# Two layer borders: four weight tiles held on either side and multiplied with one half of the tokens, then the other

## The chip, the core and the metric

One core of one Trainium2 chip runs the whole program. The metric is the device time of one execution in microseconds. TensorE (PE; its weight loads are listed as PEld), VectorE (DVE), ScalarE (ACT), GpSimd (POOL) and the queue of SyncE (SP) each work through their own instructions in order and wait for one another on semaphores.

## The reference

Four layers work in fp32 on one batch of S = 256 tokens of width D = 2048. What matters here is what stands between the output product of one layer and the input product of the next:

```
layers 0 and 1:   h = layernorm(x) * (1 + scale) + shift;   p = h @ w_in[l]
                  y_f = fourier_mix(u_f) * silu(z_f);       y_a = mla_attention(...) * silu(z_a)
                  y = concat([y_f, y_a]) @ w_out[l]
                  x = layernorm(ALPHA * x + gate * y, ln_g[l], ln_b[l])
layer 2 (even):   p = rms_norm(x, even_norm) @ even_w_in;   ...   x = x + y @ even_w_out
layer 3 (odd):    p = rms_norm(x, odd_norm) @ odd_w_in;     ...   x = x + y @ odd_w_out
```

So two norms follow one another behind layer 0 (the closing layernorm, then the opening one of layer 1), and two behind layer 1 (the closing layernorm, then the rms norm of layer 2). A token's norms need that token's 2048 values only.

## The kernel before

The token block lies in X as two halves of 128 tokens, t = 0 and t = 1. A weight matrix streams through in jobs: each is one tile of 256 rows by 512 columns (512 KB), loaded into one of 9 staging tiles `stg` by the SP queue. A "split" makes of it a high part `whi` (ACT, a rounding copy to fp32r; 4 buffers, NSPLIT) and a low part `wlo` (DVE, the difference). PE then takes three products per tile, high·high, high·low and low·high (fp32r), and adds them up in PSUM. Eight jobs q = 0..7 make one group (`group`, line 205) and run through the 2048 rows of the contraction.

Units of kind A (first groups of a layer) keep a 128x128 piece of the weight in the array and stream all 256 tokens of Hh or Hl past it: 24 matmuls of 256 columns per job. Units of kind B (`w_out`) keep 128 tokens in the array and stream 512 weight columns: 12 matmuls per job, 6 for each half of the tokens. Hh and Hl are the high and low part of the transposed, normed input.

The order is written by `Plan`. `run` (line 174) prepares job i (load and split are put into the queues) and then issues the matmuls of job i - 3 (AHEAD). Every engine takes the steps of that one list, in its order, and skips those that are not its own.

At a border, in the order of the list:

- `out` of the last group (line 2136): for t = 0 and then 1 the PSUM result times the gate, plus ALPHA·x, then bn_stats, on DVE.
- `post_norm` (lines 381, 1775, 1783, 2111): the aggregate and a reciprocal square root by three Newton steps on small columns, for both halves together (`meanvar`, `rsqrt`), then for each half three DVE passes over X. Behind layer 0 ACT meanwhile computes sum and sum of squares of half 0; behind layer 1 it squares both halves.
- `ln` or `rms` (lines 2072, 2091): the statistics of the next norm, both halves together.
- `xn` (lines 1766, 2099): the normed values by quarters of 512 columns, half 0 on DVE, half 1 on ACT, into XN, which lies over Z.
- `trans` (lines 346, 1734, 2049): PE transposes 2 x 2 blocks of 128x128 for both halves (line 1533); scale and shift are applied from PSUM on ACT or DVE, ACT writes Hh, DVE writes Hl.
- `lead` (line 992) puts this first part with three transposed steps in front of the first job of the next layer, and one more transposed step (`more`) in front of each of its jobs 1 to 5. The first eight jobs are "fresh": their products with Hh come first, and those with Hl last.

The steps `ln_load`, `mla_begin` and `even_begin` put DMAs into POOL's queue; they are not changed.

Of the kernel before, what the change touches and what calls it, by code (L numbers as in the profile page):

```python
# [16 lines left out]
D = 2048  # L17
S = 256
KT = D // 128
EPS = 1e-6  # L20
# [9 lines left out]
AHEAD = 3  # L30
WINDOW = 6
# [10 lines left out]
PT2X = dict(even=(IQ, IQ + 384), odd=(V3 + 512, KS3 + 512))  # L42

# [18 lines left out]
class Plan:  # L62
# [3 lines left out]
    def __init__(self):  # L66
# [9 lines left out]
        self.starting = True  # L76
        self.retired = []
# [78 lines left out]
    def prep(self, job):  # L156
        slot, free = self.stgs.get()
        while not self.starting and slot >= NSTG:
            self.retired.extend(free)
            slot, free = self.stgs.get()  # L160
# [4 lines left out]
        if job["mode"] == "split":  # L165
            hi, hfree = self.his.get()
            job["hi"] = hi
            a, b = self.tick("hi"), self.tick("lo")
            self.step("split", slot=slot, n=job["n"], hi=hi, ld=ld, hfree=hfree, hi_done=a)
            job["split"] = b  # L170
        elif job["mode"] == "ada":
            job["dve"](job)

    def run(self):
        n = len(self.jobs)
        held, weights = [], 0
        for i in range(n + AHEAD):
# [6 lines left out]
            if i < n:  # L184
                if job.get("last_chunk"):
                    self.starting = False
                self.prep(job)
                held.append(job)
# [3 lines left out]
            while weights > AHEAD or self.starting and len(held) > AHEAD:  # L192
# [12 lines left out]
    def group(self, cols, units, post, pre=None, late=None, early=None):  # L205
        g = {}
        n = sum(c[2] for c in cols)
        for q in range(8):
# [5 lines left out]
            def body(job, q=q):  # L214
                if q == 0:
                    g["pair"], g["free"] = self.pairs.get()
                tok = self.tick("mm")
                here = early is not None and q < 2
                self.step("mm", q=q, early=early if here else None, pair=g["pair"], free=g["free"] if q == 0 else (), split=job["split"],
                          hi=job["hi"], slot=job["slot"], units=units, h=[self.y_early[q]] * 2 if here else [self.h[2 * q], self.h[2 * q + 1]],  # L220
                          h_hi=[self.h_hi[2 * q], self.h_hi[2 * q + 1]] if job.get("fresh") else None)
                self.his.put(job["hi"], tok)
                self.stgs.put(job["slot"], tok)
                g["mm"] = tok
# [9 lines left out]
            self.jobs.append(dict(mode="split", src=src, n=n, mm=body, pre=pre if q == 0 else late if q == 3 else None,  # L234
# [126 lines left out]
    def ln(self, x, post=None):  # L361

        s = dict(mv=self.small(4), v=self.small(2), y=self.small(2), nb=self.small(1), t=self.small(2), nbt=self.tick("nb"))
        self.step("ln", x=x, post=post, **s)
        self.norm = dict(how="ln", ready=s["nbt"], y=s["y"], mv=s["mv"], nb=s["nb"], nm=post["nm"] if post else None)
# [15 lines left out]
    def post_norm(self, l):  # L381
        tk = [self.tick("post_norm") for _ in range(4)]
        s = dict(l=l, ln=self.ln_in, x=self.x[1, 3], mv=self.small(4), v=self.small(2), y=self.small(2), t=self.small(2),
                 z_free=self.z_free, out=tk)
        if l == 0:
            s.update(sum=self.small(1), nm=self.small(1), sq=self.small(1))
            s["summed"], s["mean"], s["squared"] = self.tick("pn_sum"), self.tick("pn_mean"), self.tick("pn_sq")
        else:
            s["ss"] = self.small(4)
            for _ in range(4):  # L390
                s["squared"] = self.tick("sumsq")
        self.ar = (tk[3],)
        self.h_free = self.mm_last
        return self.step("post_norm", **s)
# [48 lines left out]
    def out_post(self, l, g):  # L443
        def post(pair, mm):
            free = []
            for t in range(2):
                a = self.tick("out_in")
                free.append(a)
                s = dict(l=l, g=g, t=t, pair=pair, mm=mm)
                if l < 2:  # L450
# [5 lines left out]
                    self.x[t, g] = st  # L456
                elif l == 2:
# [11 lines left out]
    def w_out(self, l, w):  # L469
        for g in range(4):  # L470
            def late(g=g):
                if g == 0:
                    self.y_rest()
                    if l < 2:
                        self.ln_in = self.tick("ln_landed", 32)
                        self.step("ln_load", l=l, scores=("score_mm", self.count["score_mm"]))
                    if l == 2:
                        self.toep = self.tick("toep_landed", 96)
                        self.step("toep_windowed", logits=("sm_logit", self.count["sm_logit"]), pool=self.pool_mm)
            self.group([(w, g * 512, 512)], B2, self.out_post(l, g), late=late, early=l)  # L480
# [534 lines left out]

    def whole(self):
# [58 lines left out]
        def norm1():  # L1075
            p = self.post_norm(0)
            self.ln(p["out"][3], p)

        n1 = self.lead(norm1, lambda qs: self.mod_h(1, qs), lambda: self.mla(1))
# [6 lines left out]
        def norm2():  # L1086
            p = self.post_norm(1)
            self.rms(p["squared"], p["ss"], 4)

        self.lead(norm2, lambda qs: self.transposed("en", None, qs), self.even)  # L1090
# [48 lines left out]
def build(nc, A):  # L1139
    with ExitStack() as ctx:  # L1140
# [18 lines left out]
        whi = [sb(f"whi{i}", [128, 2, 512], F32R) for i in range(NSPLIT)]  # L1159
        X = sb("X", [128, 2, D])  # L1160
# [8 lines left out]
        for whole, tiles in ((AR, stg), (ARL, wlo)):  # L1169
            tiles += [whole[:, 3072 + i * 1024:4096 + i * 1024].rearrange("p (k n) -> p k n", k=2) for i in range(EXTRA)]  # L1170
        RX = sb("RX", [128, 768])
# [181 lines left out]
        def tensor(e):  # L1353
# [7 lines left out]
            for kind, s in plan.order:  # L1361
                if "bank" in s and kind != "setup":
                    B = PB[s["bank"]]
                if kind == "mm":
# [51 lines left out]
                    ins.then_inc(SEM["mm"], 1)  # L1416
                elif kind == "direct" and s["split"] is None:
# [285 lines left out]
        def scalar(e):  # L1703
# [7 lines left out]
            for kind, s in plan.order:  # L1711
# [54 lines left out]
                elif kind == "xn":  # L1766
# [3 lines left out]
                    if s["how"] == "ln":  # L1770
                        ins = act(XN[:, 1, cols], X[:, 1, cols], ACT.Identity, bias=sm(s["nb"], 1), scale=sm(s["y"] + 1, 1))
# [3 lines left out]
                elif kind == "post_norm" and s["l"] == 0:  # L1775
# [7 lines left out]
                elif kind == "post_norm":  # L1783
                    q.wait_ge(s["z_free"])
                    for n in range(4):
                        t, cols = n // 2, slice(1024 * (n % 2), 1024 * (n % 2) + 1024)
# [659 lines left out]
```

## Time and profile before

| | |
|---|---|
| median of 3 runs | 1639.75 us (1638.62 to 1642.59) |
| profiled execution | 1637.07 us, its span 1635.3 us |
| PE busy | 1508.8 us (92%) |
| DVE busy | 1086.4 us (66%) |
| ACT busy | 706.7 us (43%) |
| mean granted clock of TensorE | 0.965 of full speed |

The profiled execution has its own time, a little below the median; a sum from its rows is made against 1637.07 us. Times of rows are counted from the start of the span. A matmul's listed duration (0.28 us, say) includes its way through the array; how often one starts is read from the difference of two starts.

### The profile page before, as it was taken

How to read it: one execution, taken by the hardware profiler on the slowest of the kernel's cores; microseconds unless marked ns; L12 is line 12 of the kernel's file. 1: busy time of each engine (PE TensorE's matmuls, PEld its weight loads, DVE VectorE, ACT ScalarE, POOL GpSimd, SP SyncE). 2: the span in 40 equal slices, each digit the busy share in tenths (PEclk: the TensorE clock that was granted, in tenths of full speed). 3: DMA queues.
4: the chain of work that ended last, by engine and by line, in shares of the span. 5: the costliest groups of instructions: out<-in, count | busy, mean ns of one | idle time of the engine just before them, and what ended most of it. 6: DMA issues, size and time to landing. Idle time of an engine off the chain costs nothing.

```text
span 1635.3 us, 25215 instructions
## 1 busy us (share of the span) xinstructions
PE 1508.8 (92%) x9919; PEld 1329.6 (81%) x9919; DVE 1086.4 (66%) x1854; ACT 706.7 (43%) x1195; POOL 30.7 (2%) x56
## 2 busy tenths in 40 slices
PE   4888999989949999999968999999998999999998
PEld 0667788988839888998858998789987998879986
DVE  3426668889987757666676466884655667886553
ACT  1324234335326444444325344544544545655442
POOL 3000000000000000000000000010000000000000
PEclk8898999999979999999988999999999999999999
DMA  9996887998945766676546546427665553434662
GB/s 351 380 380 230 256 288 252 368 330 331 346 155 170 255 168 200 226 244 207 193 141 197 174 142 177 133 73 262 184 193 153 167 155 104 115 106 140 183 218 90
DMA packets 182437, 345.00 MB, mean 211 GB/s; under 512 B 28876, under 2 KB 43440, under 8 KB 181552
## 3 DMA queue, kind: packets, MB, share of 16 engines
q1 hardware_dynamic: 177744, 326.88, 61.7%
q0 software_dynamic: 4576, 16.52, 2.9%
q8 instruction: 78, 1.28, 0.3%
q14 instruction: 39, 0.32, 0.1%
HBM read 341.16 MB, written 2.20 MB: 210 GB/s over the span
## 4 chain that ended last, share of the span: by engine, by line
PE 78%; DVE 8%; DMA 5%; ACT 4%; issue 3%; SPq 2%; POOLq 0%; POOL 0%; DVEq 0%; ACTq 0%
PE PM L1359 65%; PE PB L1359 8%; DMA stg<-in_w_in 3%; SPq L1284 2%; ACT AR L1709 2%; DMA AR<-in_w_in 1%; ACT whi L1709 1%; DVE X L1934 1%; PE PB L1561 1%; PE PB L1533 1%; DVE AC L1934 1%; PE PB L1636 1%; DMA AR<-in_w_ada 1%; DVE wlo L2010 1%; DVE AR L1934 1%
## 5 line engine op out<-in xcount | busy, mean ns | idle before, releaser
L2010 DVE TENSOR_TENSOR wlo<-stg,whi 128x1024 fp32r<-128x1024 f32 (+2 forms) x421 | 500.1, 1197 | 350.3 <-ACT whi L1709 349.0
L1709 ACT ACTIVATE whi<-stg 128x1024 fp32r<-128x1024 f32 (+2 forms) x421 | 434.2, 1037 | 467.4 <-PE PM L1359 352.2
L1359 PE MATMUL PM<-Hh,whi 128*128 128x256 f32 x1824 | 528.0, 292 | 9.1 <-DVE wlo L2010 6.6
L1359 PE MATMUL PM<-Hh,wlo 128*128 128x256 f32 x1780 | 501.5, 285 | 0.0
L1359 PE MATMUL PM<-Hl,whi 128*128 128x256 f32 x1824 | 498.1, 285 | 0.0
L1359 PEld LDWEIGHTS PM<-Hh,whi 128*128 128x128 f32 x1824 | 353.2, 194 | 28.8 <-issue 12.4
L1359 PEld LDWEIGHTS PM<-Hh,wlo 128*128 128x128 f32 x1780 | 344.1, 193 | 0.0
L1359 PEld LDWEIGHTS PM<-Hl,whi 128*128 128x128 f32 x1824 | 343.1, 193 | 0.6
L1359 PE MATMUL PM<-whi,Hh 128*128 128x512 f32 (+1 forms) x576 | 224.3, 391 | 0.0
L1359 PE MATMUL PM<-wlo,Hh 128*128 128x512 f32 (+1 forms) x576 | 220.9, 385 | 0.0
L1359 PE MATMUL PM<-whi,Hl 128*128 128x512 f32 (+1 forms) x576 | 219.1, 385 | 0.0
L1934 DVE SCALAR_TENSOR_TENSOR AC<-stg,CA,AC 128x1024 f32<-128x1024 f32 x120 | 153.7, 1281 | 9.3 <-DMA stg<-in_w_ada 7.2
L1359 PEld LDWEIGHTS PM<-whi,Hh 128*128 128x128 f32 x576 | 108.9, 189 | 22.2 <-issue 0.7
L1359 PEld LDWEIGHTS PM<-wlo,Hh 128*128 128x128 f32 x576 | 108.8, 189 | 20.8 <-issue 0.2
L1359 PEld LDWEIGHTS PM<-whi,Hl 128*128 128x128 f32 x576 | 107.4, 189 | 22.0
L1359 PE MATMUL PM<-whi,ARL 128*128 128x512 f32 (+1 forms) x272 | 86.0, 383 | 0.0
L1709 ACT ACTIVATE AR<-PB 128x384 f32<-128x384 f32 (+2 forms) x104 | 45.7, 478 | 91.9 <-PE PB L1636 31.1
L1359 PE MATMUL PB<-AR 64*128 64x256 f32 (+4 forms) x576 | 72.8, 359 | 5.0 <-ACT AR L1709 4.5
L1533 PE MATMUL PB<-IDN,Z 128*128 128x128 f32 x128 | 24.1, 333 | 57.4 <-DVE Z L2105 26.5
L1533 PEld LDWEIGHTS PB<-IDN,Z 128*128 128x128 f32 x128 | 18.5, 172 | 60.5 <-DVE Z L2105 26.7
L1359 PEld LDWEIGHTS PB<-AR 64*128 64x128 f32 (+2 forms) x576 | 47.3, 174 | 22.8 <-issue 7.9
L1359 PEld LDWEIGHTS PM<-whi,ARL 128*128 128x128 f32 x272 | 51.1, 188 | 10.0
(268 smaller groups left out, 1461.3 us busy)
## 6 DMA issues: line engine op xcount, KB each, us to landing
stg<-in_w_ada SPq DMA_DIRECT2D x162, 512.0 KB, 6.5
stg<-in_w_in SPq DMA_DIRECT2D x107, 512.0 KB, 5.4
stg<-in_even_w_in SPq DMA_DIRECT2D x80, 512.0 KB, 3.6
stg<-in_odd_w_in SPq DMA_DIRECT2D x72, 512.0 KB, 3.7
stg<-in_w_out SPq DMA_DIRECT2D x64, 512.0 KB, 5.0
stg<-in_even_w_out SPq DMA_DIRECT2D x32, 512.0 KB, 3.9
stg<-in_odd_w_out SPq DMA_DIRECT2D x32, 512.0 KB, 4.2
AR<-in_w_ada SPq DMA_DIRECT2D x30, 512.0 KB, 11.5
```

The lines of the kernel that those rows point to most:

```text
L1284: e.dma_start(dst, src).then_inc(SEM[f"landed{slot}"], 16)
L1359: return e.matmul(out, l, r, start=start, stop=stop, skip_group_check=True)
L1533: ins = e.transpose(B[:, kk * S + t * 128:kk * S + t * 128 + 128], XN[:, t, k * 128:(k + 1) * 128], IDN[:, :])
L1561: ins = e.matmul(B[:, 0:S], ar(UU + t * 1024 + s["g"] * 128, 128), CSS[:, t, :], start=t == 0, stop=t == 1)
L1636: ins = e.transpose(B[:, n * 128:(n + 1) * 128], L[:, n * 128:(n + 1) * 128], IDN[:, :])
L1709: return e.activation(out, x, f, **k)
L1934: return e.scalar_tensor_tensor(out=out, in0=in0, scalar=scalar, in1=in1, op0=op0, op1=op1)
L2010: e.tensor_tensor(wlo[s["slot"]][:, :, 0:n], stg[s["slot"]][:, :, 0:n], whi[s["hi"]][:, :, 0:n].bitcast(F32), ALU.subtract).then_inc(SEM[" ...
```

## The change

At the borders behind layers 0 and 1:

- In the last group of `w_out` the jobs 4 to 7 multiply with half 0 alone (`units[0:1]`), and their four tiles stay held. When job 7 has done so, the four are multiplied with half 1. The `out` steps of the two halves wait for different matmuls, and each half has its own `post_stat` and `post_norm`.
- The first four jobs of the next layer do no 256-column products. `first_half` multiplies them with half 0 of Hh, then (all four) with half 0 of Hl, then transposes half 1, multiplies all four with half 1 of Hh, and with half 1 of Hl: 192 matmuls of 128 columns instead of 96 of 256. Transposed steps 4 and 5 are issued inside, 6 and 7 in front of jobs 4 and 5.
- `lead_halves` replaces `lead`: `half_xn` and `half_trans` cover 512 columns of one half. For half 0 ACT writes XN, Hh, and a second copy into TMP from which DVE makes Hl; for half 1 DVE writes XN and reads PSUM itself.
- `half_norm` computes the next norm's statistics of one half at a time.
- From job 3 of `w_out`'s first group until job 7 of the next layer four more `whi` buffers (in ARL) and two more staging tiles (in AR, with their `wlo` in ARL) are in use. Behind job 7 of the last group the matmuls are issued one job later than usual (`later`).

In the last group of `w_out` of layers 2 and 3 job 7 alone is done this way (hold=1), and `out` of half 0 waits for its first part.

```diff
+            while not self.border and hi >= NSPLIT:
+                hi, hfree = self.his.get()
...
-            while weights > AHEAD or self.starting and len(held) > AHEAD:
+            while weights > AHEAD + (held[0]["later"] if held and "later" in held[0] else 0) or self.starting and len(held) > AHEAD:
...
+                    return self.first_half(job, q, g, units)
...
+                if q < 8 - hold:
+                    self.his.put(job["hi"], tok)
+                    self.stgs.put(job["slot"], tok)
+                else:
+                    g["held"].append((job, s))
+                if hold and q == 7:
+
+                    first = tok
+                    for job, s in g["held"]:
+                        tok = self.tick("mm")
+                        self.step("mm", **{**s, "units": units[1:2]})
+                        self.his.put(job["hi"], tok)
+                        self.stgs.put(job["slot"], tok)
+                    g["mm"] = [first, tok]
+                else:
+                    g["mm"] = tok
                 self.mm_last = tok
 
...
+        self.step("post_stat", **s)
+        if t == 1:
+            self.half_norm(0)
+        self.step("post_norm", **s)
+        h["out", t] = out
...
+        h = self.half
+
+        def part(job, q, t, lo):
+            tok = self.tick("mm")
+            self.step("mm_half", q=q, t=t, lo=lo, pair=g["pair"], free=g["free"] if q == 0 and t == 0 and not lo else (),
+                      split=job["split"], hi=job["hi"], slot=job["slot"], units=units, h=h["lo" if lo else "hi", t, q // 2])
+            return tok
+
+        g["held"].append((job, q))
+        part(job, q, 0, False)
+        if q < HELD - 1:
+            return
+        for j, k in g["held"]:
+            part(j, k, 0, True)
+        self.half_trans(1, 0)
+        self.half_trans(1, 1)
+        for j, k in g["held"]:
+            part(j, k, 1, False)
+        self.more(4)
+        for j, k in g["held"]:
+            tok = part(j, k, 1, True)
+            self.his.put(j["hi"], tok)
+            self.stgs.put(j["slot"], tok)
+        self.more(5)
+        self.mm_last = g["mm"] = tok
 
 
 
...
-                s = dict(l=l, g=g, t=t, pair=pair, mm=mm)
+                s = dict(l=l, g=g, t=t, pair=pair, mm=mm[t] if g == 3 else mm)
...
+                    if g == 3:
+                        self.post_norm(l, t)
...
+                        self.border = True
+                        self.his.free = [f for f in self.his.free if f[0] < NSPLIT]
+                        self.stgs.free = [f for f in self.stgs.free if f[0] < NSTG + EXTRA]
+                        for i, at in enumerate(HI_MORE[l]):
+                            self.his.put(NSPLIT + 4 * l + i, *idle)
+                        for i in range(len(STG_MORE)):
+                            self.stgs.put(NSTG + EXTRA + i, *idle)
...
+                       hold=0 if g < 3 else HELD if l < 2 else 1)
...
+        def lead():
+            l, h = self.half["l"], self.half
+            self.half_xn(0, 0)
+            self.half_trans(0, 0)
+            self.half_xn(0, 1)
+            self.half_trans(0, 1)
+            self.half_norm(1)
+            self.half_xn(1, 0)
+            self.half_xn(1, 1)
+            self.norm = dict(how="ln" if l == 0 else "rms", ready=h["tok"][1], y=h["y"], mv=h["mv"], nb=h["nb"])
+            self.more = more
+            begin()
+
+        def more(q):
+            if q % 2 == 0:
+                self.normed((q // 2,))
+            trans((q,))
+            if q == 7:
+                self.zw = self.h[KT - 1]
+        self.jobs[n]["pre"] = lead
+        for q in range(8):
+            self.jobs[n + q]["half" if q < HELD else "fresh"] = True
+        for q in (4, 5):
+            self.jobs[n + q]["pre"] = lambda q=q: more(q + 2)
+        self.jobs[n + 7]["border_end"] = True
+        return n
+
     def whole(self):
...
+                    for kk in range(2):
+                        k = 2 * s["q"] + kk
+                        opened = set()
+                        for u in s["units"]:
+                            b = PM[2 * s["pair"] + u["bk"]]
+                            first = k == 0 and s["t"] == 0 and not s["lo"] and u["bk"] not in opened
+                            opened.add(u["bk"])
+                            out = b[0:u["n"], u["off"] + s["t"] * 128:u["off"] + s["t"] * 128 + 128]
+                            wh, wl = (W[:, kk, u["c0"]:u["c0"] + u["n"]] for W in (H, L))
+                            if s["lo"]:
+                                ins = mm(out, wh, Hl[:, k, tk], False, False)
+                            else:
+                                mm(out, wh, Hh[:, k, tk], first, False)
+                                ins = mm(out, wl, Hh[:, k, tk], False, False)
+                    ins.then_inc(SEM["mm"], 1)
+                elif kind == "half_trans":
...
+                    for j in range(4):
+                        ins = affine(Hh[:, 4 * s["c"] + j, tk], j)
+                    ins.then_inc(SEM["h_hi"], 1)
+                    if s["t"] == 0:
+                        q.wait_all(s["tfree"])
+                        for j in range(4):
+                            ins = affine(TMP[s["tmp"]][:, j * 128:(j + 1) * 128], j)
+                        ins.then_inc(SEM["tr_half_act"], 1)
...
+                elif kind == "post_norm" and s["l"] == 1:
+                    t = s["t"]
...
+                    for n in range(2):
+                        cols = slice(1024 * n, 1024 * n + 1024)
...
+                        act(XN[:, t, cols], X[:, t, cols], ACT.Square, accum_out=sm(s["ss"] + 2 * t + n, 1)).then_inc(
+                            SEM["sumsq"], 1)
...
+                elif kind == "half_trans":
+                    T, k0, tk = TMP[s["tmp"]], 4 * s["c"], slice(s["t"] * 128, s["t"] * 128 + 128)
+                    q.wait_ge(s["hh"])
...
+                        ins.then_inc(SEM["tr_half_dve"], 1)
+                    q.wait_ge(s["aff"])
+                    q.wait_ge(s["h_free"])
+                    e.tensor_tensor(Hl[:, k0:k0 + 4, tk], T[:, :].rearrange("p (k s) -> p k s", k=4),
+                                    Hh[:, k0:k0 + 4, tk].bitcast(F32), ALU.subtract).then_inc(SEM["h_lo"], 1)
```

The lines that are left out of the diff are the new buffers' places, the small columns of the statistics, and the DVE code of `post_stat`, `half_norm` and `half_xn`, which does on one half what `meanvar`, `ln`, `rms` and `xn` did on two.

## Rows read from the trace of the kernel before

**Rows 1.** The page, section 1: busy us, share of the span, instructions.
```profile
PE 1508.8 (92%) x9919; PEld 1329.6 (81%) x9919; DVE 1086.4 (66%) x1854; ACT 706.7 (43%) x1195; POOL 30.7 (2%) x56
```

**Rows 2.** PE's waits: engine, line, waited for; total us, times, longest.
```profile
PE PB L1533 <- DVE Z L2105: 26.5, 4, 20.9
PE PB L1533 <- DVE Z L2109: 22.7, 2, 22.5
```

**Rows 3.** Stretches: length; PE, PEld, DVE, ACT, POOL busy; clock, DMA share, GB/s.
```profile
462.80:468.20 5.40, 5.40 (x24) 4.13 (x22) 2.02 (x4) 1.06 (x1) 0.00 (x0) 1.00 0.67 225
468.20:490.70 22.50, 0.03 (x2) 0.04 (x1) 21.20 (x45) 5.00 (x6) 0.90 (x1) 0.58 0.18 54
490.70:495.50 4.80, 4.80 (x23) 4.78 (x24) 2.84 (x6) 3.38 (x7) 0.00 (x0) 0.50 0.00 0
495.50:519.80 24.30, 24.11 (x203) 23.94 (x203) 19.25 (x25) 15.15 (x22) 0.00 (x0) 1.00 0.56 161
...
867.60:893.10 25.50, 25.03 (x211) 24.86 (x211) 18.16 (x24) 15.45 (x23) 0.00 (x0) 1.00 0.70 218
```

**Rows 4.** Timeline of DVE behind layer 0: start, duration, what.
```profile
468.26 0.69 DVE L2144 TENSOR_TENSOR TMP<-PM,GT 128x512 f32<-128x512 f32 x1 [0.34 <-PE PM L1359]
...
472.49 0.39 DVE L1996 BATCH_NORM_AGGREGATE SM<-STA 128x2 f32<-128x24 f32 x2
...
475.17 9.65 DVE L1934 SCALAR_TENSOR_TENSOR X<-X,SM,AR 128x2048 f32<-128x2048 f32 x6
484.85 2.47 DVE L2077 BATCH_NORM_STATS2 STA<-X 128x6 f32<-128x512 f32 x4
...
490.00 1.00 DVE L2109 TENSOR_SCALAR Z<-X,SM 128x512 f32<-128x512 f32 x2
```

**Rows 5.** Timeline of ACT behind layer 0.
```profile
480.12 1.91 ACT L1709 ACTIVATE Z<-X 128x2048 f32<-128x2048 f32 x1 [13.46 <-DVE X L1934]
...
484.30 0.19 ACT L1709 ACTIVATION_READ_ACCUMULATOR Z<-X,SM 128x1 f32 x1
490.00 1.52 ACT L1709 ACTIVATE Z<-X,SM 128x512 f32<-128x512 f32 x2 [5.51 <-DVE SM L1934]
491.81 1.02 ACT L1709 ACTIVATE Hh<-PB,MOD 128x256 fp32r<-128x256 f32 x2 [0.30 <-PE PB L1533]
```

**Rows 6.** Timeline of ACT behind layer 1.
```profile
860.20 1.06 ACT L1709 ACTIVATE Z<-X 128x1024 f32<-128x1024 f32 x1
...
863.88 1.33 ACT L1709 ACTIVATE Z<-X,SM 128x512 f32<-128x512 f32 x2 [2.54 <-DVE SM L1934]
865.59 0.84 ACT L1709 ACTIVATE Hh<-PB,VEC 128x256 fp32r<-128x256 f32 x2 [0.38 <-PE PB L1533]
```

**Rows 7.** Timeline of PE: matmuls that stream 1, 128 and 256 columns.
```profile
460.78 1.84 PE L1359 MATMUL PB<-ONE,AC 128*128 128x1 f32 x16
...
490.69 2.79 PE L1533 MATMUL PB<-IDN,Z 128*128 128x128 f32 x12 [22.47 <-DVE Z L2109]
...
498.16 0.28 PE L1359 MATMUL PM<-Hh,wlo 128*128 128x256 f32 x1
498.28 0.28 PE L1359 MATMUL PM<-Hh,whi 128*128 128x256 f32 x1
...
507.44 0.60 PE L1533 MATMUL PB<-IDN,Z 128*128 128x128 f32 x4
```

**Rows 8.** Weight loads by shape, whole span: count, busy us, mean ns, idle.
```profile
L1359 PEld LDWEIGHTS PM<-Hh,whi 128*128 128x128 f32 x1808 | 350.8, 194 | 28.8 <-issue 12.4 <-DVE wlo L2010 11.5 <-DVE ARL L2010 4.3
...
L1359 PEld LDWEIGHTS PB<-AR 128*64 128x64 f32 x192 | 11.8, 136 | 7.4 <-issue 1.7 <-DVE AR L1934 0.7
```

**Rows 9.** Timeline of ACT and DVE: the split of one tile in layer 1.
```profile
500.91 1.05 ACT L1709 ACTIVATE whi<-stg 128x1024 fp32r<-128x1024 f32 x1
...
501.98 1.23 DVE L2010 TENSOR_TENSOR wlo<-stg,whi 128x1024 fp32r<-128x1024 f32 x1 [0.26 <-ACT whi L1709]
```

**Rows 10.** Timeline of DVE at the end of the kernel.
```profile
1628.60 1.29 DVE L2151 TENSOR_TENSOR X<-PM,X 128x512 f32<-128x512 f32 x2 [8.50 <-PE PM L1359]
```

More of the change, by code:

```diff
@@ L157, in prep @@
         slot, free = self.stgs.get()
-        while not self.starting and slot >= NSTG:
-            self.retired.extend(free)
+        while not self.starting and NSTG <= slot < NSTG + EXTRA or not self.border and slot >= NSTG + EXTRA:
+            if slot < NSTG + EXTRA:
+                self.retired.extend(free)
             slot, free = self.stgs.get()
@@ L203, in run, with group @@
                     self.round()
-    def group(self, cols, units, post, pre=None, late=None, early=None):
-        g = {}
+    def group(self, cols, units, post, pre=None, late=None, early=None, hold=0):
+        g = dict(held=[])
         n = sum(c[2] for c in cols)
@@ L232, in done @@
                     self.pair_put(g["pair"], *free)
-            self.jobs.append(dict(mode="split", src=src, n=n, mm=body, pre=pre if q == 0 else late if q == 3 else None,
+            self.jobs.append(dict(mode="split", src=src, n=n, mm=body, later=1 if hold == HELD and q == 7 else 0, pre=pre if q == 0 else late if q == 3 else None,
                                   post=done if q == 7 else None))
@@ new lines, in half_norm, with half_xn @@
+    def half_norm(self, t):
+        h = self.half
+        h["tok"][t] = self.tick("nb")
+        self.step("half_norm", t=t, l=h["l"], y=h["y"], nb=h["nb"], mv=h["mv"], nm=h["nm"], sq=h["sq"], ss=h["ss"],
+                  squared=h.get("squared") if h["l"] == 0 else h["squared", t], out=h["out", t],
+                  v=self.small(1), w=self.small(1))
+    def half_xn(self, t, c):
+        h = self.half
+        self.step("half_xn", t=t, c=c, l=h["l"], y=h["y"], nb=h["nb"], mv=h["mv"], ready=h["tok"][t], z_free=self.z_free)
+        h["xn", t, c] = self.tick(f"half_xn{t}")
@@ new lines, in half_trans @@
+    def half_trans(self, t, c):
+        h = self.half
+        b, fr = self.now(self.banks)
+        mm = self.tick("tr_mm")
+        i, ifree = self.now(self.tmps)
+        hh = self.tick("h_hi")
+        a = self.tick("tr_half_act") if t == 0 else self.tick("tr_half_dve")
+        lo = self.tick("h_lo")
+        need = [self.mod[1, 4 + c], self.mod[1, c]] if h["l"] == 0 else []
+        self.step("half_trans", t=t, c=c, how="mod" if h["l"] == 0 else "en", bank=b, free=fr, src=h["xn", t, c], mm=mm, tmp=i,
+                  tfree=ifree, need=need, aff=a, hh=hh, h_free=self.h_free)
+        self.banks.put(b, a)
+        self.tmps.put(i, lo)
+        h["hi", t, c], h["lo", t, c] = hh, lo
```

199 lines of the change are left out of this document (138 added, 61 removed).

## The prediction

> **What bounds the kernel now.** The page first: PE is busy for 92% of the span, DVE for 66% [rows 1]. So time is won only where PE stands still, and lost where PE gets more to do. The list of waits then says where PE stands still: two waits on the normed input, 22.5 us behind layer 0 and 20.9 us behind layer 1 [rows 2]. The table by stretches shows both sides of the first: DVE busy for 21.2 of 22.5 us, PE not at all, and behind it the first eight jobs of the next layer packed: PE busy for 24.1 of 24.3 us and for 25.0 of 25.5 us [rows 3]. The reader is to see that such a wait is one chain on DVE, and that there is no slack behind it into which more PE work could go. The clock falls in the wait, and is back at full 4.8 us after PE resumes.
>
> **How I count.** F is the moment at which job 7 of `w_out`'s last group has done half 0. The pass of half 1 over four tiles is 24 matmuls of 512 columns, 5.4 us [rows 3], so PE's last old work ends at F+5.4, where it ends today. The weights don't hold it up: with eight `whi` buffers the splits run ahead. A split takes 1.05 us on ACT and 1.23 on DVE [rows 9], a tile now 1.36 us of PE; this edit I price at nothing, and at up to 2 us a border if DVE is late with one.
>
> **The first half's chain, layer 0.** DVE: `out` of half 0 takes half of 468.26 to 472.49, 2.15. Aggregate and Newton steps take 472.49 to 475.17, 2.7 for both halves; these are tiny columns, so one half costs nearly the same, 2.5. Three passes over X: half of 9.65, 4.85 [rows 4]. That is F+9.5. ACT's sum and square then take 480.12 to 484.49, 4.4 [rows 5]; DVE meanwhile does `out` and `post_stat` of half 1, to F+14.15. `half_norm(0)`, 2.5: F+16.7. XN by ACT, 0.76: F+17.5. So PE waits 12.1 us instead of 22.5. But its next two steps are both transposes, and the second needs XN of the second quarter, which ACT writes only after four copies to Hh and four to TMP. A copy of 256 columns takes 0.5 us here [rows 5], of which I give 0.35 to one of 128. From 490.69, the first transpose, to 491.81, the first copy, are 1.1 us. So F+17.5 + 1.1 + 8 x 0.35 + 0.8 = 22.2; the first four transposes end at F+18.4 (0.21 each), so there is a new wait of 3.9 us between the two groups of four. Products start at F+23, T+17.5 if T is the end of the old work; today at T+24.9.
>
> **Layer 1 is worse.** Here ACT squares both halves, and the squares of half 1 stand in its queue ahead of `half_xn(0, 0)`. They wait for DVE's last pass over X: F+14.15 + 2.4 (`half_norm(0)`) + 4.85 = 21.4, and the last one takes 1.06 [rows 6] and a read of 0.19 [rows 5]: F+22.7. Behind this wait stands all that ACT has for the new layer: XN, both sets of copies, the splits of jobs 4 to 6. XN 0.67: F+23.4. PE waits 18.0 us, today 20.9, and then 3.5 between the transposes (1.1 + 8 x 0.32 + 0.67, less 0.85 of transposing).
>
> **More PE work.** Each border has 192 matmuls of 128 columns for 96 of 256. One of 256 starts each 0.12 us [rows 7]. None of 128 in fp32r is in the trace. The lower bound is proportion: 0.053 for the columns at 2.4 GHz and the 0.013 that the 256 show above theirs, 0.067. The upper one is a start each 0.213, as 128-column transposes do at the low clock: (2.79 - 0.45) / 11 [rows 7]. The nearest rows say 0.11: 16 matmuls of one column take 1.84 us, so that an almost empty one still costs 0.105 to 0.112, and four transposes of 128 columns start 0.109 apart [rows 7]. The load of the array explains it: 128 columns of weights take 58 ns longer than 64 [rows 8], so about 0.116 for all 128, and each of the 192 loads another piece. With 256 columns the load hides under the stream, with 128 it no longer can. I take 0.112: 192 x 0.112 - 96 x 0.12 = 21.5 - 11.5 = +10.0 us a border. The Trainium skill ("TensorE: Matmul & The Clock Gate", section "Back-to-back issue gap") gives about 81 ns for a stream of load and matmul at N = 128. By that the term would be +4.0; no row here shows 81, and those that come near show 105 to 112.
>
> **New waits inside.** (a) Between the transposes of half 1 and their copy to Hh: 0.27 + 4 x 0.35, less 0.44 for the second four, 1.2 us (layer 1: 1.1). (b) Step 6 stands in front of job 4, behind the split of job 7 in the list, and PE has nothing left but it. Behind step 5's transposes come on ACT the scale and shift (0.95), Hh (0.6), the split of job 7 (1.05), XN; on DVE Hl, the split (1.2), XN (0.54): 0.3 + 0.95 + 0.6 + 1.05 + 1.2 + 0.54 = 4.6 us (layer 1: 4.4), after which PE can transpose for job 4. Nothing on PE covers it. (c) DVE does Hl of half 0, `half_norm(1)` (484.85 to 490.00, 5.15 [rows 4]) and two XN to F+33.1; PE comes for them at F+35, so they are hidden, by about 2 us. With faster matmuls they would not be. The splits of jobs 4 to 6 on DVE (3.5 us) and a first `ada` product end before Hl of half 1 is wanted.
>
> **Clock.** It falls in any wait of this length here; today about 20 matmuls run at the low clock per border, then about as many (8 transposes, 14 narrow ones, at 0.213). Difference nothing; if it doesn't come back, rival C.
>
> **The other edits.** The DMAs keep their order; POOL's wait for the last X, now T+16 against T+17. The held tiles free their staging late, but eleven exist: jobs 7 and on have theirs 20 us early. At the ends of layers 2 and 3 `out` of half 1 no longer stands behind that of half 0: 1.29 us for two [rows 10], 0.6 gained at each, -1.2.
>
> **Sum.**
> - Layer 0: waits 12.1 + 3.9 + 1.2 + 4.6 = 21.8, today 22.5 + 0.2; work +10.0: +9.1.
> - Layer 1: waits 18.0 + 3.5 + 1.1 + 4.4 = 27.0, today 20.9 + 0.5; work +10.0: +15.6.
> - Ends: -1.2.
> Together +23.5: from 1637.07 to 1660.6 us in the profiled execution's terms. The median is 2.7 above that execution: 1663.3, say 1663.
>
> **Rivals.**
> A, the forecast, +23.5: 70%, its own range 1653 to 1673.
> B, a narrow matmul costs by its columns, 0.067. Against it the one-column row; for it, that no fp32r one is shown. Work falls to +1.4 a border, but PE then outruns DVE: about 2 us more of wait (c), 1 of Hl. Layer 0 +3.2, layer 1 +7.2, ends -1.2: +9.2, 1649. 14%. By the 81 ns of the Trainium skill (same page and section) it would be about +13, 1653.
> C, the narrow ones start each 0.213, because the clock stays low under them or for another reason. The 12 transposes and 23 matmuls after 490.7 did raise it [rows 3]. 2 x (192 - 14) x 0.1 = +36: 1699. 6%.
> D, faster. The place is the inside waits: 3.9, 1.2, 4.6 and 3.5, 1.1, 4.4, 18.7 us in all. If the steps that I put behind one another in ACT's queue (second copy, split, XN) are over before PE asks, and the columns alone count (work +2.8 instead of +20): 23.5 - 18.7 - 17.2 = -12.4: 1627 by the median. With all waits gone it decides from 0.10 us a matmul down. For it: these waits rest on my reading of one list; against: all are in one engine's order. 5%.
> E, the two sides cancel, 1640: half of D. 5%.
>
> **Numbers.** What a measurement of this kernel tells from no change is about 0.3%, 5 us. Faster: D's 5 and 1 of E, 6%; same: the other 4 of E and 1 of B, 5%; slower 89%. The range takes in B and large parts of A's misses above, and leaves out C and D: 1644 to 1680.
>
> **What would show it.** PE's first wait behind layer 0 near 12 us and behind layer 1 near 18, each followed by one of about 4 between two groups of transposes; narrow matmuls 0.11 apart, with PEld nearly full; a wait of about 4.5 us in front of step 6's transposes. I am wrong if these start 0.07 apart, if ACT's XN of half 0 behind layer 1 comes before its squares of half 1, or if the clock stays at half.

## The result, and the profile after

The changed kernel takes 1703.4 us (median of 4 runs, 1701.4 to 1704.1), the one before 1641.2 in the same comparison (1638.6 to 1642.7): ratio 1.038, interval 1.036 to 1.040. I had forecast 1663 with a range of 1644 to 1680. The direction is right, the size is 40 us off, and the time is that of rival C (1699), to which I had given 6%.

The head of the page of the kernel after, to be laid beside [rows 1]: PE has 63 us more of busy time (1572.2 for 1508.8), nearly all of the 65 us by which the span is longer.

```profile
span 1700.7 us, 25673 instructions
## 1 busy us (share of the span) xinstructions
PE 1572.2 (92%) x10111; PEld 1390.7 (82%) x10111; DVE 1092.1 (64%) x1908; ACT 712.7 (42%) x1225; POOL 30.7 (2%) x56
```

The list of PE's waits of the kernel after, first behind layer 0 (460 to 540 us), then behind layer 1 (865 to 960); columns: us in total, times, longest. They answer to [rows 2].

```profile
PE PB L1572 <- ACT Z L1866: 15.8, 2, 12.0
PE PB L1690 <- DVE Z L2343: 4.5, 1, 4.5
PE PM L1488 <- ACT Hh L1866: 0.7, 1, 0.7
...
PE PB L1572 <- ACT Z L1866: 20.4, 2, 17.4
PE PB L1690 <- DVE Z L2341: 4.3, 1, 4.3
PE PM L1488 <- ACT Hh L1866: 0.4, 1, 0.4
```

So behind layer 0 PE waits 12.0, 3.8, 0.7 and 4.5 us (forecast 12.1, 3.9, 1.2, 4.6), behind layer 1 17.4, 3.0, 0.4 and 4.3 (forecast 18.0, 3.5, 1.1, 4.4). The waits aren't where the 40 us are. The table by stretches of the kernel after shows where; its columns are the stretch, its length, busy us of PE, PEld, DVE, ACT, POOL with their instructions, the granted clock, DMA share, GB/s. Layer 0's border: the products of half 0, those of half 1, the wide jobs behind them. Then the same three behind layer 1. Beside [rows 3].

```profile
485.10:508.30 23.20, 22.46 (x106) 22.06 (x106) 10.56 (x25) 7.52 (x17) 0.00 (x0) 0.50 0.08 22
509.50:530.50 21.00, 20.95 (x99) 20.55 (x98) 4.75 (x10) 1.25 (x3) 0.00 (x0) 0.50 0.20 51
535.90:549.00 13.10, 13.10 (x103) 13.10 (x103) 7.65 (x10) 4.71 (x7) 0.00 (x0) 0.92 0.36 105
...
895.20:917.90 22.70, 22.32 (x106) 21.92 (x105) 7.09 (x20) 6.46 (x17) 0.00 (x0) 0.50 0.28 94
918.80:939.90 21.10, 21.10 (x100) 20.79 (x99) 4.34 (x10) 1.03 (x2) 0.00 (x0) 0.50 0.17 50
945.20:958.50 13.30, 13.30 (x104) 13.30 (x104) 5.94 (x7) 5.25 (x8) 0.00 (x0) 0.91 0.42 119
```

The clock is 0.50 (1.2 GHz) under all narrow products, 99 in 21.0 us: one each 0.212, where the forecast had 0.112. It is at the low level from 469.8 for 68 us and from 876.0 for 72 us; before, for 24 and 21 us. It returns only under the wide products, as the timeline of PE in the kernel after shows (start, us, line, operation):

```profile
486.20 0.41 PE L1488 MATMUL PM<-Hh,ARL 128*128 128x128 f32 x1
486.41 0.41 PE L1488 MATMUL PM<-Hh,wlo 128*128 128x128 f32 x1
...
534.98 1.09 PE L1690 MATMUL PB<-IDN,Z 128*128 128x128 f32 x4 [4.53 <-DVE Z L2343]
535.72 0.56 PE L1488 MATMUL PM<-Hh,whi 128*128 128x256 f32 x1
...
537.57 0.41 PE L1488 MATMUL PM<-Hh,whi 128*128 128x256 f32 x1
537.78 0.41 PE L1488 MATMUL PM<-Hh,wlo 128*128 128x256 f32 x1
...
538.30 0.28 PE L1488 MATMUL PM<-Hh,whi 128*128 128x256 f32 x1
538.42 0.28 PE L1488 MATMUL PM<-Hh,wlo 128*128 128x256 f32 x1
```

Narrow products (128 streamed columns) and wide ones (256) start equally far apart at the low clock, 0.21. The clock is back at 538.1, 2.4 us after the first wide one, and the starts are 0.12 apart again.

### The profile page after: what moved, and what is told of

Its sections match the earlier page's. It is cut to its first block, busy times and chain, and to the rows that moved or that the text cites. A ratio compares the mean times of both kernels' runs of the same rounds, so it can differ in the third digit from the quotient of the medians.

```text
span 1700.7 us, 25673 instructions
## 1 busy us (share of the span) xinstructions
PE 1572.2 (92%) x10111; PEld 1390.7 (82%) x10111; DVE 1092.1 (64%) x1908; ACT 712.7 (42%) x1225; POOL 30.7 (2%) x56
## 4 chain that ended last, share of the span: by engine, by line
PE 77%; DVE 8%; DMA 5%; ACT 5%; issue 3%; SPq 2%; POOLq 0%; POOL 0%; DVEq 0%; ACTq 0%
PE PM L1488 64%; PE PB L1488 8%; DMA stg<-in_w_in 3%; SPq L1413 2%; ACT AR L1866 2%; ACT whi L1866 1%; DVE AC L2125 1%; DVE X L2125 1%; PE PB L1690 1%; PE PB L1718 1%; DVE wlo L2201 1%; DMA stg<-in_w_out 1%; PE PB L1793 1%; DMA AR<-in_w_in 1%; DMA AR<-in_w_ada 1%
## 5 line engine op out<-in xcount | busy, mean ns | idle before, releaser
L2201 DVE TENSOR_TENSOR wlo<-stg,whi 128x1024 fp32r<-128x1024 f32 (+2 forms) x382 | 452.5, 1194 | 319.8 <-ACT whi L1866 319.1
L1866 ACT ACTIVATE whi<-stg 128x1024 fp32r<-128x1024 f32 (+2 forms) x382 | 393.4, 1036 | 414.3 <-PE PM L1488 317.4
L1488 PE MATMUL PM<-Hh,whi 128*128 128x256 f32 (+2 forms) x1792 | 525.8, 295 | 9.4 <-DVE wlo L2201 7.5
L1488 PE MATMUL PM<-Hh,wlo 128*128 128x256 f32 (+1 forms) x1804 | 525.2, 292 | 0.0
L1488 PE MATMUL PM<-Hl,whi 128*128 128x256 f32 (+2 forms) x1792 | 496.6, 287 | 0.0
L1488 PEld LDWEIGHTS PM<-Hh,whi 128*128 128x128 f32 (+1 forms) x1792 | 352.2, 197 | 29.2 <-DVE wlo L2201 12.6
L1488 PEld LDWEIGHTS PM<-Hl,whi 128*128 128x128 f32 (+1 forms) x1792 | 341.9, 196 | 0.6
L1488 PEld LDWEIGHTS PM<-whi,Hl 128*128 128x128 f32 x520 | 96.9, 189 | 19.7
L1488 PE MATMUL PM<-Hh,ARL 128*128 128x128 f32 (+1 forms) x180 | 61.7, 378 | 1.1 <-ACT Hh L1866 1.1
L1488 PE MATMUL PM<-whi,ARL 128*128 128x512 f32 (+1 forms) x176 | 55.5, 380 | 0.0
L1488 PE MATMUL PM<-wlo,ARL 128*128 128x512 f32 (+1 forms) x140 | 52.8, 377 | 0.0
```

The source lines that it names most:

```text
L1488: return e.matmul(out, l, r, start=start, stop=stop, skip_group_check=True)
L1866: return e.activation(out, x, f, **k)
L2201: e.tensor_tensor(wlo[s["slot"]][:, :, 0:n], stg[s["slot"]][:, :, 0:n], whi[s["hi"]][:, :, 0:n].bitcast(F32), ALU.subtract).then_inc(SEM[" ...
```

## Experiments

Theory: the waits and the price at the full clock were right, and narrow matmuls that start at the low clock leave it low. Rivals: 0.112 is wrong; the clock is kept down by the waits inside the border; the cost isn't PE's at all. Below, a kernel's extra time is counted against the kernel before as timed with it: the changed kernel has +62.2 us.

**1. The narrow matmul at the full clock.** In the kernel before, the second group of layer 2 (PE busy without a break) is multiplied in halves, with all 128 stationary columns in one kernel and 64 in the other; with 64, half of that group's outputs is left out.

```diff
+m = s["narrow"]                                 # 128 or 64
+for x, w in ((xh, wh), (xl, wh), (xh, wl)):
+    for h in range(2):
+        o, th = u["off"] + 128 * h, slice(128 * h, 128 * h + 128)
+        ins = mm(b[0:m, o:o + 128], w[:, 0:m], x[:, kk, th], ...)
```

> The kernel before, with one change far from the borders: in the second group of layer 2 (eight jobs, PE packed and at full clock today, 192 matmuls of 256 columns starting 0.12 us apart, 23.0 us) each product is done as two matmuls of 128 columns, 384 in all. Theory 1 (the load of the array sets the price, and the clock, once full, stays): a start each 0.112 us, 43.0 us, +20 us. Theory 1b (same price, but such matmuls also bring a full clock down): the stretch begins at 0.112 and goes over to 0.213, the granted clock falls within it, up to +59 us. Theory 2 (128 columns in fp32r cost 0.213 at any clock): 0.213 from the first one at granted clock 1.0, +59 us. Theory 3 (the columns count): 0.067, +3 us.

> As narrow_warm, but each of the 384 matmuls loads only 64 of the 128 weight columns, so half of this group's outputs aren't computed. Same number of matmuls and of streamed columns, half the load. If the load sets the price (theory 1): a start each 0.067 us or so, 26 us for the group, +3 us against before. If 128 streamed columns are slow by themselves: as narrow_warm, 0.11 or 0.213.

Measured: 1657.3 against 1637.2, ratio 1.013 (1.010 to 1.015), +20 us for 384 narrow ones in place of 192 wide; with 64 stationary columns 1638.1, ratio 1.000 (0.998 to 1.001). Stretches of the first kernel, then the timeline of the first and of the second:

```profile
895.00:914.00 19.00, 19.00 (x173) 19.00 (x172) 4.90 (x4) 4.01 (x4) 0.00 (x0) 1.00 0.22 45
914.00:938.00 24.00, 24.00 (x216) 24.00 (x216) 3.00 (x4) 4.07 (x7) 0.00 (x0) 1.00 0.19 39
```

```profile
914.78 0.39 PE L1359 MATMUL PM<-Hh,wlo 128*128 128x128 f32 x2
915.00 0.38 PE L1359 MATMUL PM<-Hh,whi 128*128 128x128 f32 x2
```

```profile
914.97 0.28 PE L1359 MATMUL PM<-Hh,wlo 128*64 128x128 f32 x2
915.08 0.28 PE L1359 MATMUL PM<-Hh,whi 128*64 128x128 f32 x2
```

A pair each 0.22, so 0.111 a narrow matmul, and 0.06 with half the stationary columns: the load sets the price, as the forecast had it. The clock stays at 1.00 for the 43 us of the narrow ones. The price of 0.112 stands, and with it the first rival falls.

**2. The changed kernel at the full clock.** 50 and 16 extra matmuls of 512 columns fill the first and second wait behind layer 0, 74 and 13 those behind layer 1; the transposes overwrite their result.

```diff
+hi, split, n = s["fill"]
+q.wait_ge(split)
+for _ in range(n):
+    mm(B[:, :], whi[hi][:, 0, 0:128], whi[hi][:, 0, :], True, True)
 q.wait_ge(s["src"])
```

> The changed kernel, with matmuls of 512 columns on a held weight tile put into PE's waits in front of the transposes of half 0 (50 and 16 behind layer 0, 74 and 13 behind layer 1; their result is overwritten by the transposes). They only keep PE busy. Theory 1: the clock is full when the narrow matmuls begin and stays there, these start 0.112 apart, and the time is what the prediction worked out, about 1660 us, less some 2 us a border for the slow starts that both kernels have. Theory 1b: it begins so and falls under them, 1670 to 1700. Theory 2 (narrow costs 0.213 at any clock): 1703 as it is.

Measured: 1657.7 against 1637.2, ratio 1.0135 (1.0115 to 1.0154). Stretches: the filled wait and the first products behind layer 0, and the filled wait behind layer 1.

```profile
466.30:478.50 12.20, 11.64 (x53) 9.35 (x52) 11.28 (x32) 5.12 (x6) 0.00 (x0) 1.00 0.31 101
485.00:498.00 13.00, 11.84 (x106) 11.60 (x106) 11.14 (x27) 7.61 (x16) 0.00 (x0) 1.00 0.09 32
...
849.00:867.00 18.00, 17.34 (x77) 14.04 (x77) 15.08 (x33) 5.20 (x9) 1.69 (x3) 1.00 0.26 87
```

The clock stays at 1.00 until 511, behind the last narrow product of layer 0's border, and until 897 at the other. PE does more work, and the kernel is 42 us nearer to the one before (+20.5 for +62.2). These +20.5 are close to the +23.5 of the sum.

**3. Wide products in halves.** The changed kernel with the operands' roles exchanged in the border: 128 tokens stationary, 512 weight columns streamed, 48 matmuls a border. Their result then has another layout, so what is computed from it is wrong; the order of the steps is that of the changed kernel.

```diff
-mm(out, wh, Hh[:, k, tk], first, False)
-ins = mm(out, wl, Hh[:, k, tk], False, False)
+mm(out, Hh[:, k, tk], H[:, kk, :], k == 0, False)
+ins = mm(out, Hh[:, k, tk], L[:, kk, :], False, False)
```

> The changed kernel with the same passes over the four held tiles at each border, but the operands' roles exchanged: 128 tokens stay in the array and 512 weight columns stream, 12 matmuls of 512 columns a tile instead of 48 of 128. The sums of these four tiles come out in another layout than the rest of their group, so the values behind are wrong; time, order and waits are those of the changed kernel. Theory 1: the clock comes back some 4 to 7 us into the first pass as it did before the change, the passes cost 11 us a border instead of 41, DVE's part becomes visible by 2 to 3 us, and the time is 1646 to 1655 us. If the passes' order or the held buffers and not the narrow matmuls were what keeps the clock low, it stays above 1685.

Measured: 1649.5 against 1637.2, ratio 1.0083 (1.0067 to 1.0100). The clock falls in the waits and comes back each time: under the first stretch at 487.8, 2.5 us behind the first product, as one starts each 0.43 us at first and then each 0.23. Mean clock of the first stretch of products and of the second:

```profile
485.00:495.00 10.00, 7.18 (x27) 5.59 (x26) 5.83 (x20) 5.74 (x11) 0.00 (x0) 0.84 0.19 52
498.00:507.00 9.00, 8.33 (x32) 6.30 (x32) 7.42 (x16) 2.46 (x6) 0.00 (x0) 0.81 0.07 11
```

The waits on ACT's XN are those of the changed kernel (36.2 us in four, longest 17.4, in both lists); one on DVE of 2.9 us is new, as expected. 50 us are gone (+12.3 for +62.2). Not all of that is the clock: at the full clock 48 products each 0.227 are 10.4 us a border less than 192 each 0.111, 21 us for two; the other 29 are what the clock costs, as far as this run tells.

**4. Packed narrow products at the low clock, without the change.** The kernel before, its chain and waits untouched, with only the first four tiles' products of both borders narrow; a second kernel with 64 of 128 stationary columns (half of these outputs left out).

```diff
+m = min(u["n"], s["narrow"])                    # narrow: 128 or 64
+for t in range(2):
+    mm(b[0:m, u["off"] + t * 128:u["off"] + t * 128 + 128], w[:, 0:m], Hh[:, k, t * 128:t * 128 + 128], ...)
```

> The kernel before, its chains and its 22.5 and 20.9 us waits as they are, but the products of the first four tiles behind layers 0 and 1 in 192 matmuls of 128 columns a border for 96 of 256 (same tiles, same order, no break between them). Theory 1: narrow matmuls that start at the low clock don't lift it, so it stays at 0.5 from the wait until the 256-column ones of the fifth tile have run for 2 to 3 us. Then 192 x 0.213 = 40.9 us for the 13.7 us that 23 x 0.213 + 73 x 0.12 take now, +27 a border, and some 1.2 us for 12 wide ones at the low clock: +28 a border, +56 in all, about 1693. Rival: in the changed kernel the clock stayed down because the block is broken by waits (4.0, 1.0, 4.7 us); here the block is packed, so the clock is back about 5 us after the work resumes, and a border costs 24 x 0.1 less 23 x 0.09 for the low part and 10 us for the rest: +10 to +11 a border, 1657 to 1660.

> The kernel before with its first four tiles' products behind layers 0 and 1 in 192 matmuls of 128 columns, as in the run with the packed narrow block, but with 64 of 128 stationary columns (so half of these outputs is left out). If the load of 128 stationary columns is what leaves the clock low, it comes back as in the kernel before, a start each 0.06, and the time is 1635 to 1640 where before takes 1638. If 128 columns of stream are too few by themselves, the clock stays low behind at least one border: 192 x 0.11 = 21 for 13.7 and 1.2 for the tail, +8.6 a border, 1647 (one border) to 1655 (both).

Measured with 128 stationary columns: 1654.0 in one execution, 1678.8, 1678.8 and 1680.1 in three, where before takes 1638.7. So +15 once and +40 three times, with a mean granted clock of 0.973 once and of 0.954 to 0.959 three times. The profiled one (1680.1) shows how they can differ. Stretches: the narrow block and the first wide products behind layer 0, then the narrow block behind layer 1.

```profile
493.90:537.20 43.30, 43.30 (x207) 43.30 (x206) 13.04 (x19) 11.01 (x17) 0.00 (x0) 0.50 0.14 43
537.90:541.00 3.10, 3.10 (x17) 3.10 (x16) 2.13 (x3) 0.90 (x2) 0.00 (x0) 0.50 0.49 127
541.00:548.00 7.00, 7.00 (x59) 7.00 (x59) 4.71 (x6) 3.52 (x6) 0.00 (x0) 0.97 0.52 154
898.60:922.00 23.40, 23.40 (x207) 23.40 (x206) 11.74 (x18) 10.25 (x16) 0.00 (x0) 0.97 0.51 166
```

The same block of the same program, PE busy from end to end in both: 43.3 us at one border, where the clock never rose under it, 23.4 at the other, where it was back 3.9 us after PE resumed with 12 transposes. So breaks aren't needed to keep the clock low, and the rival of the waits inside falls. Neither expectation holds whole: I had +56 for "it never lifts" and +21 for "it always lifts", and got +40 or +15. From the first transposes behind layer 0 to those behind layer 1 this execution takes 31.0 us longer than the kernel before (404.7 for 373.7), and from there to the end 11.0 (781.9 for 770.9): a low border costs 20 us more than one where the clock returns. The 1654.0 has no trace; that both its borders rose is an inference from its time and clock, and by the trace two such borders would cost 22, not 15.

With 64 stationary columns: 1636.4, ratio 1.000 (0.999 to 1.001), before 1637.7. The profiled execution, first products behind layer 0 and then those behind the rise of the clock:

```profile
495.11 0.41 PE L1360 MATMUL PM<-Hh,whi 128*64 128x128 f32 x2
495.32 0.41 PE L1360 MATMUL PM<-Hh,wlo 128*64 128x128 f32 x2
...
502.56 0.28 PE L1360 MATMUL PM<-Hh,whi 128*64 128x128 f32 x2
502.67 0.28 PE L1360 MATMUL PM<-Hh,wlo 128*64 128x128 f32 x2
```

At the low clock one starts each 0.107, half of the 0.213 with 128 columns, so there too the load sets the price. The clock returned at 497.4 and 869.3, 5.7 and 3.8 us after PE resumed. All 10 executions lie between 1633.3 and 1641.5, where I had reckoned 8.6 us for a border that stays low; so probably none did. With 128 stationary columns three of four did. That the load of all 128 is what leaves the clock low is likely by this, but not shown: one border with this load rose, and the two kernels ran on different chips.

**5. A kick.** The changed kernel with 16 extra matmuls of 512 columns, or 32 transposes of 128, in front of the first narrow product of each border.

```diff
+if s["q"] == s["t"] == 0 and not s["lo"]:
+    for _ in range(16):
+        mm(PM[2 * s["pair"]][:, :], H[:, 0, 0:128], H[:, 0, :], True, True)
...                                              # in the second kernel:
+    for _ in range(32):
+        e.transpose(PM[2 * s["pair"]][:, 0:128], IDN[:, :], IDN[:, :])
```

> The changed kernel with 16 extra matmuls of 512 columns (result unused) in front of the first narrow product of each border, behind both waits on the transposes; all waits are as in the changed kernel. Theory: what keeps the clock low is that narrow matmuls don't lift it, though they hold it once it is up. The 16 take up to 6.9 us at the low clock, lift it, and the 192 narrow ones then start 0.112 apart for 0.213: -19.4 + 6 to 7, and some 1.5 less in low transposes and in the wide ones behind: -14 a border, 1675 where the changed kernel took 1703. Rival: narrow matmuls between waits of 1 and 4.7 us can't hold it either: it falls back inside the block, and the time is 1703 + 12 less a part, 1695 to 1716.

> As the kernel with 16 wide matmuls, but 32 transposes of 128 columns of fp32 in their place (0.213 each at the low clock, 6.8 us). They start as far apart as the narrow products do. [...] Then they lift it, as the 12 in front of the products in the kernel before may do: 1675. Theory 2: any instruction that starts each 0.213 leaves the clock low: then 1703 + 13.6 = 1717.

Measured: 1679.6, ratio 1.0248 (1.0234 to 1.0262), and 1677.0 (1672.5 to 1688.8), ratio 1.0256 (1.0219 to 1.0293), before at 1637.7. Stretches behind layer 0: with wide kicks the kick, the narrow products of half 0, the 1.2 us in which PE waits for Hh, the products of half 1; then with transposes the kick and the products of half 0.

```profile
486.00:491.00 5.00, 5.00 (x20) 4.08 (x20) 1.76 (x3) 4.76 (x11) 0.00 (x0) 0.76 0.35 102
491.00:501.90 10.90, 10.90 (x100) 10.90 (x99) 8.55 (x22) 0.98 (x2) 0.00 (x0) 1.00 0.01 2
502.60:503.80 1.20, 0.14 (x1) 0.14 (x2) 0.16 (x1) 1.20 (x4) 0.00 (x0) 1.00 0.00 0
505.80:523.70 17.90, 17.90 (x86) 17.90 (x86) 4.05 (x9) 0.63 (x1) 0.00 (x0) 0.50 0.20 53
```

```profile
486.60:492.30 5.70, 5.70 (x33) 5.70 (x32) 2.42 (x5) 5.42 (x11) 0.00 (x0) 0.58 0.33 91
492.40:502.60 10.20, 10.20 (x94) 10.20 (x92) 7.79 (x20) 0.22 (x1) 0.00 (x0) 1.00 0.01 2
```

Both kicks lift it, the transposes at 491.3, 4.7 us behind the first of them. Extra work of 5 to 6 us halves the time of the 96 products behind it and brings the kernel 20 and 23 us nearer to the one before (+41.9 and +39.3 for +62.2); I had expected 28 (1675 for 1703). In the profiled run with wide kicks part of that is lost because the clock fell again at 505.5, 1.8 us after the small wait for Hh, and the 86 narrow ones behind it didn't bring it back, 0.1 us each. In the profiled run with transposes it didn't fall under either narrow block, and that one took 1673.0; two of its other three took 1681.0 and 1688.8, and no trace shows why. My rival (they can't hold it past a wait) is right for layer 0's border under the wide kick, and wrong for the one behind layer 1, where it stood at 1.00 from 891.2 to 921.8.

**6. The w_out side alone.** The change's held last tiles and its `out`, statistics and post norm by halves; the next layer's norm, transposes and products as before, 256 wide. In a second kernel the norm of half 0 is no step of its own but one with half 1's. In both the matmuls are no longer issued one job later (`later`).

```diff
-            self.half_xn(0, 0)
-            self.half_trans(0, 0)
...
-            self.half_xn(1, 1)
...
+        n = self.lead(norm, trans, layer, fill)   # norm: half_norm(1); then both halves at once
...
-        if t == 1:
-            self.half_norm(0)                     # these two in the second kernel only
```

> The change's w_out side alone: the last four tiles of layers 0 and 1 (one tile in layers 2 and 3) are held and multiplied with half 0, then half 1, and each half's out, statistics and post norm start when it is done; the next layer's norm and its first products are for both halves at once, 256 columns wide, as before. By the chain that the prediction wrote (F+14.15 for half 1's out and statistics, +2.5 half_norm of half 0, +4.85 for three passes, +5.15 for the last norm), PE's wait behind layer 0 is 21.3 us for 22.5; behind layer 1, with the last square and 2.5 of norm behind F+21.5, 19.8 for 20.9; the ends of layers 2 and 3 give 1.2. Sum -3.5: ratio 0.998, 1633.5 on a chip where before takes 1637. Rival: splitting the small steps over halves eats it (the extra 2.5 of half 0's statistics and 2.5 of its norm are longer in fact) or DVE's work on half 0 makes it late with the tiles' splits: no gain, 1637 to 1640.

> The w_out side alone, as in the run that kept this side, with the next layer's norm of half 0 no longer in a step of its own between half 1's statistics and its three passes (2.4 us on DVE, 476.2 to 478.6 in that run's trace) but in one step with half 1's, as wide as before. Nothing on PE hides these 2.4 us, since the chain is on DVE alone: the wait behind layer 0 falls from 21.5 to 19.1, that behind layer 1 from 19.7 to 17.4. -4.7 more in all: 1629 where before takes 1638.6, ratio 0.9945. Rival: behind layer 1 the last square on ACT and the chain behind it set the end, and only layer 0 gains: 1631, ratio 0.996.

Measured: 1633.6 against 1638.7, ratio 0.9973 (0.9962 to 0.9985), and 1631.0 against 1637.7, ratio 0.9953 (0.9940 to 0.9965). The longest waits, of the first kernel (behind layer 1, behind layer 0) and of the second:

```profile
PE PB L1669 <- DVE Z L2320: 24.3, 2, 19.7
PE PB L1669 <- DVE Z L2322: 22.3, 2, 21.5
```

```profile
PE PB L1667 <- DVE Z L2314: 22.9, 4, 17.8
PE PB L1667 <- DVE Z L2316: 19.3, 1, 19.3
```

Behind layers 0 and 1, 22.5 and 20.9 became 21.5 and 19.7 (forecast 21.3 and 19.8), then 19.3 and 17.8 (19.1 and 17.4). Both versions beat the kernel before, if by half a per cent at most, and the changed one by far. The second is the better by its waits; the intervals of the two ratios just overlap.

**7. The clock held in the kernel before.** 95 and 87 extra wide matmuls in its two waits; and 90 and 83 in the first kernel of 6.

```diff
+hi, split, n = s["fill"]
+q.wait_ge(split)
+for _ in range(n):
+    mm(B[:, :], whi[hi][:, 0, 0:128], whi[hi][:, 0, :], True, True)
...                                              # then the transposes of the first XN
```

> The kernel before with 95 wide matmuls of 512 columns into a bank that the next transposes overwrite, put in front of the first transposes behind layer 0, and 87 behind layer 1 (extra work, its result unused); at 0.227 us they fill 21.6 of 22.5 and 19.7 of 20.9 us. Theory: the clock stays at full, so the 12 transposes take 1.35 us for 2.79 and the some 23 products that now start 0.213 apart start 0.12 apart: 1.4 + 2.1 = up to 3.5 us less a border, as far as the copies behind the transposes allow: -4 to -7 in all, 1630 to 1633 where before takes 1637. Rival: the first products are paced by ACT's and DVE's copies and not by the clock, or the fill makes PE late: -2 to +1.

> hold_out and the fill together (90 and 83 fillers for the shorter waits). If both work and add: -3.5 and -4 to -7, 1626.5 to 1629.5 where before takes 1637, ratio 0.9935 to 0.9955; it would beat both kernels. If hold_out brings nothing: as fill_before.

Measured: 1637.6 against 1638.7, ratio 0.9993 (0.9981 to 1.0005), where the rival came true; and 1633.6, ratio 0.9972 (0.9962 to 0.9982), which is no more than the held side alone and short of the 0.9935 to 0.9955 expected. The list of waits of the kernel before with the fill, behind layer 0 (460 to 500):

```profile
PE PB L1542 <- DVE Z L2118: 2.2, 2, 1.4
PE PM L1363 <- ACT Hh L1718: 0.3, 1, 0.3
```

The clock stayed at 1.00 through both borders, but PE then waits for DVE's XN and ACT's copies: the last of the border's transposes starts 42.5 us behind T for 42.9 before, 0.4 us a border (T is the end of the old work, as in the prediction). I had counted 3.5, and too much at that: of the 23 matmuls at the low clock in [rows 3] 12 are the transposes, so 11 products run slow and the sum was 2.4. In the kernel before, what the low clock costs is thus nearly all hidden behind DVE's and ACT's work; in the changed one nothing hides it.

## Why the prediction was wrong

- The step that failed is **Clock**: "today about 20 matmuls run at the low clock per border, then about as many (8 transposes, 14 narrow ones, at 0.213). Difference nothing". All 192 ran at 0.213, and the clock came back only in the wide ones behind. The step rested on [rows 3], where PE resumes with 12 transposes and then wide products, and the clock is back 4.8 us later. The change has neither there: 8 transposes in two groups with a wait between, then narrow products. Experiments 2, 3 and 5 give 20 to 50 us back by touching nothing but what PE does in the wait or in the border. That 14 narrow products would be enough was taken over from the wide ones; no row showed a narrow product at all.
- **More PE work** was right at the clock that it assumed: 0.111 for 0.112 (experiment 1). Rival B is out (and its sum left out, behind layer 1, the 3 us of further waits that it names). So is the 81 ns of the Trainium skill ("TensorE: Matmul & The Clock Gate", section "Back-to-back issue gap"): no run here shows it, for fp32r with 128 stationary columns.
- **The first half's chain, Layer 1 is worse, New waits inside**: all eight waits came out below the forecast, by 0.1 to 0.7 us, together 46.1 for 48.8. D's hope of waits that vanish had nothing for it.
- **The other edits**: the held side works as counted, -1.0 and -1.2 us in PE's waits where it is alone (experiment 6). At the ends, PE's wait behind layer 2 is 4.6 us for 5.1, and DVE's last step is one of 0.70 for two of 1.29 together: 0.5 and 0.6 for the 0.6 each of the forecast.
- **Rival C** had the mechanism and nearly the size: 2 x (192 - 14) x 0.1 = 36 on top of 1663. By borders, with T as in the prediction: the next group of products starts at T+81.7 behind layer 0 and at T+85.9 behind layer 1, before at T+51.6 and T+49.6, so +30.1 and +36.3. My terms with the measured waits are 9.1 - 0.8 = 8.3 and 15.6 - 1.9 = 13.7; 178 x 0.101 = 18.0 comes on top at each, and some 3.1 for the 20 later transposes and the first 11 wide ones at the low clock: 29.4 and 34.8. The other 2.2 us of both borders I haven't placed. I gave C 6% because "the 12 transposes and 23 matmuls after 490.7 did raise it", which says nothing of narrow ones (and counts the 12 twice, as above).

Left open: why the clock rose under the packed narrow block at one border and not at the other, though both had the same 12 transposes before it and waits of 22.5 and 20.9 us; and whether it would at times rise in the changed kernel too. By their times (1701.4 to 1704.1) it did in none of its four runs; one has a trace.

## What to carry to other kernels

A wait that drops TensorE's clock can cost more than its length: ask what PE does first behind it, and price that work at 1.2 GHz for all of its length unless a row shows that this very form of matmul brought the clock back. Halving the streamed columns while the stationary tile keeps its 128 columns doubles the loads; that is paid even at the full clock (0.111 for 128 columns, 0.12 for 256) and, behind a wait, can leave the clock low for the whole block. When a change buys an earlier start with more and smaller matmuls, take its two sides apart: here the side that lets DVE start earlier gives 0.3 to 0.5%, and the side that splits PE's work loses all of that and 60 us more.

## What the runs showed of the hardware

- The same narrow fp32r stream held the clock where it found it high and had no wait before or in it (1.00 for 43 us, experiment 1), and mostly didn't lift it where it found it low: in the traces it stayed at 0.50 in four places (both borders of the changed kernel, one of experiment 4 with PE busy for 43.3 us on end, one of experiment 5 after it had fallen) and came back in one.
- 128-column transposes of fp32 and narrow fp32r products both start 0.213 apart at the low clock, yet it was back 4.7 us behind the first of 32 transposes, and not under 192 narrow products in 43.3 us.
- With 64 stationary columns a 128-column product starts each 0.06 us, with 128 each 0.111; at the low clock each 0.107 and 0.213.
